# Two mixture-of-experts layers: token rows stored by chunk of channels, the second pair's token numbers by a product on chip, and another order of the last router logits

## The reference, cut to what matters

```python
group_idx = argmax(softmax(t @ w_router_group + b_group))         # one group for each token
in_group  = (t @ w_router_expert + b_expert)[group_idx]           # its 8 experts
top_p, top_i = top_k(softmax(in_group), 2)
gates = group_gate * top_p / sum(top_p)
# for each of the token's two experts e:
y[token] += gate * ((silu(x @ w_gate[e]) * (x @ w_up[e])) @ w_down[e])
```

## Time and profile before

| | |
|---|---|
| median of 3 runs | 2305.43 us (2302.77 to 2305.70) |
| profiled execution | 2309.89 us, its span 2307.7 us |
| PE busy | 2007.6 us, 87% of the span |
| mean granted TensorE clock | 0.938 of 2.4 GHz |
| chain that ended last | PE 38%, issue 32%, DMA 23%, DVE 4% |
| single largest DMA parts of it | in_w (layer 2's weights) 12%, y_rows stores 8% |

### The profile page before, as it was taken

The page is one execution under the profiler, slowest core; times in us unless marked ns, Lnnn a source line. Parts: engine busy times, 40 slices in busy tenths (PEclk is TensorE's granted clock), DMA queues, the critical chain, the costliest instruction groups (busy, mean ns, idle before and its releaser), DMA issues.

```text
span 2307.7 us, 22803 instructions
## 1 busy us (share of the span) xinstructions
PE 2007.6 (87%) x8418; PEld 1107.0 (48%) x8418; DVE 795.5 (34%) x1472; ACT 382.0 (17%) x663; POOL 80.6 (3%) x84
## 2 busy tenths in 40 slices
PE   6999998887863999999999999999988988778781
PEld 4543335554432666656557776666554322223220
DVE  3336524112114355555554554232251101111105
ACT  2335531000001122232211111111000000000000
POOL 0001010200001000000000000000001000000001
PEclk9999998899886999999999999999988998999996
DMA  7715104699986211111011214222349999999993
GB/s 223 217 38 158 55 1 146 229 419 420 419 361 197 75 55 55 45 55 51 1 62 64 80 44 155 73 73 73 128 174 332 379 427 427 427 427 426 426 411 121
DMA packets 185573, 458.47 MB, mean 199 GB/s; under 512 B 30575, under 2 KB 134767, under 8 KB 159404
## 3 DMA queue, kind: packets, MB, share of 16 engines
q1 hardware_dynamic: 171916, 441.64, 51.0%
q0 software_dynamic: 7424, 16.06, 1.9%
q10 hardware_dynamic: 6176, 0.02, 0.1%
HBM read 434.20 MB, written 32.60 MB: 202 GB/s over the span
## 4 chain that ended last, share of the span: by engine, by line
PE 38%; issue 32%; DMA 23%; DVE 4%; SPq 2%; POOL 1%; ACT 0%; DVEq 0%; POOLq 0%; ACTq 0%
DMA stream<-in_w 12%; PE bank L1522 8%; DMA y_rows<-work 8%; PE bank L1389 6%; PE bank L451 3%; PE bank L391 2%; PE bank L1527 2%; PE bank L1402 2%; PE bank L416 2%; PE bank L1564 2%; PE bank L1390 2%; PE bank L466 1%; PE bank L395 1%; SPq L1304 1%; PE bank L479 1%
## 5 line engine op out<-in xcount | busy, mean ns | idle before, releaser
L1389 PE MATMUL bank<-stream,work 128*64 128x256 f32 (+1 forms) x1072 | 379.6, 513 | 72.4 <-DMA stream<-in_w 56.5
L1390 PE MATMUL bank<-stream,work 128*64 128x256 f32 (+1 forms) x1072 | 380.1, 513 | 0.0
L1389 PEld LDWEIGHTS bank<-stream,work 128*64 128x64 f32 x1072 | 150.8, 143 | 248.1 <-issue 173.1
L1522 PE MATMUL bank<-hT,stream 128*128 128x512 f32 x512 | 230.4, 593 | 1.7 <-DVE hT L1019 1.7
L1402 PE MATMUL bank<-stream,work 128*64 128x512 f32 x736 | 192.2, 676 | 39.4 <-DVE work L1476 39.4
L1390 PEld LDWEIGHTS bank<-stream,work 128*64 128x64 f32 x1072 | 150.7, 143 | 41.3 <-issue 25.7
L1473 DVE TENSOR_TENSOR work<-bank,work 64x256 f32<-64x256 f32 (+1 forms) x68 | 37.6, 554 | 341.6 <-ACT work L1445 341.3
L1522 PEld LDWEIGHTS bank<-hT,stream 128*128 128x128 f32 x512 | 93.4, 190 | 99.9 <-issue 98.0
L1480 DVE COPY work<-bank 128x512 f32<-128x512 f32 x34 | 23.5, 692 | 325.8 <-DMA y_rows<-work 173.2
L1402 PEld LDWEIGHTS bank<-stream,work 128*64 128x64 f32 x736 | 60.6, 153 | 146.7 <-issue 121.1
L1841 PE MATMUL bank<-stream 128*128 128x256 f32 x480 | 113.1, 383 | 3.3 <-ACT work L1866 3.3
(11 more groups left out here) (358 smaller groups left out, 2550.4 us busy)
## 6 DMA issues: line engine op xcount, KB each, us to landing
stream<-in_w SPq DMA_DIRECT2D x99, 2048.0 KB, 20.2
stream<-in_w_in SPq DMA_DIRECT2D x68, 512.0 KB, 4.2
stream<-in_w_gate SPq DMA_DIRECT2D x34, 1024.0 KB, 13.3
stream<-in_w_up SPq DMA_DIRECT2D x34, 1024.0 KB, 17.7
stream<-in_w_down SPq DMA_DIRECT2D x26, 1024.0 KB, 22.5
y_rows<-work SPq DMA_DIRECT2D x136, 128.0 KB, 14.6
stream<-in_w_in SPq DMA_DIRECT2D x16, 1024.0 KB, 5.4
stream<-in_w_out SPq DMA_DIRECT2D x2, 4096.0 KB, 15.5
```

Source lines behind the costliest of these rows:

```text
L1389: pe.matmul(bank[2 + s][other:other + 64, 0:m.ff], tokens, m.wg[slot][:, k, :], start=k == 0, stop=k == KD - 1)
L1390: last = pe.matmul(bank[2 + s][mine:mine + 64, 0:m.ff], tokens, m.wu[slot][:, k, :], start=k == 0, stop=k == KD - 1)
L1522: last = pe.matmul(bank[4 + c % 2][:, :], w_hg[:, c, k, :], hT[:, k, :], start=k == 0, stop=k == KD - 1)
```

## The change

1. `x_rows` (and so `x_dram` and the gathered rows) holds the channels in the order (k, q) instead of (q, k), for channel q*8+k. All transposes and products that read it now read 128 floats side by side. DVE (layer 1) or ACT (layer 2, a new copy out of `xres`) writes it with a step of 128 floats.
2. `key` and `place` are also made for experts 2 and 3 (a second DVE operation of the same size). In the spread, after 8 products, 4 new products of one column each multiply the second half of `place` with the token numbers less 512. DVE adds 512 and casts at the end of its routing, and POOL issues the gather of pair 1 with these numbers after the fifth scatter (`FIRST_GATHER` is (1, 1)). The list then serves pairs 2 and on.
3. In layer 2, ACT copies `x_rows` and folds tiles 0 to 2; SP's store waits for ACT's copy. The logits are in the order 0, 1, 2, transposes of tile 3, logits 3. `x_rows` lies over `xg` and `xgT`, so the gather of pair 1 waits for the end of the spread there, and DVE's first copy into `xgT` for the landed stores.
4. `clear_dve` computes the token numbers, and no longer clears `xg` in layer 2.

```diff
@@ turn_rows_pe (the same slice in tokens_pe and, as stationary operand, in spread_pe)
-                    last = pe.transpose(bank[out_bank[i][h]][:, k * P:(k + 1) * P], moe1.x_rows[:, i, 4 * h + k:D:KD], ident[:, :])
+                    last = pe.transpose(bank[out_bank[i][h]][:, k * P:(k + 1) * P], moe1.x_rows[:, i, (4 * h + k) * P:(4 * h + k + 1) * P], ident[:, :])
@@ new
+        def fold_act(act, s, i):
+            for h in range(2):
+                act.wait_ge(tr_done, (s * NT + i) * 2 + h + 1)
+                act.activation(hT[:, 4 * h:4 * h + 4, i * P:(i + 1) * P],
+                               bank[4 + (i % 2) * 2 + h][:, :].rearrange("p (a b) -> p a b", a=NT), ACT.Copy).then_inc(hT_ready, 1)
@@ route_dve
-            step(dve.scalar_tensor_tensor(m.key, rank[:, :, 0:2], 1.0, m.aa[:, 0:NT, 0:2], ALU.add, ALU.mult))
-            dve.tensor_tensor(m.place, m.key.rearrange("p a b -> p (a b)").unsqueeze(2).to_broadcast([P, 2 * NT, SLOTS]),
-                              m.r_place.unsqueeze(1).to_broadcast([P, 2 * NT, SLOTS]), ALU.is_equal).then_inc(spread, 1)
+            step(dve.scalar_tensor_tensor(m.key, rank[:, :, 0:4], 1.0, m.aa[:, 0:NT, 0:4], ALU.add, ALU.mult))
+            for q in range(2):
+                dve.tensor_tensor(m.place[:, q], m.key[:, :, 2 * q:2 * q + 2].unsqueeze(3).to_broadcast([P, NT, 2, SLOTS]),
+                                  m.r_place.unsqueeze(1).unsqueeze(1).to_broadcast([P, NT, 2, SLOTS]),
+                                  ALU.is_equal).then_inc(spread, 1)
...
             dve.tensor_copy(m.blk_i[:, 0:SPARE + 1], m.blk[:, 0:SPARE + 1]).then_inc(routed, 1)
+            dve.wait_ge(*after(numbered, m.past + 1))
+            step(dve.tensor_scalar(m.first_f, bank[5][:, 0:1], float(SEQ), None, ALU.add))
+            dve.tensor_copy(m.first_i, m.first_f).then_inc(first_in[0], 1)
@@ route_pool
             for c in range(2):
                 for i in range(NT):
+                    if (c, i) == FIRST_GATHER:
+                        pool.wait_ge(*after(first_in, m.past + 1))
+                        pool.wait_ge(x_out, 16 * NT * (m.past + 1))
+                        pool.wait_ge(m.xt_done, m.past)
+                        gather_pool(pool, m, 1, m.first_i)
                     pool.indirect_dma_start(
                         out=m.list_dram, out_offset=bass.IndirectOffsetOnAxis(ap=m.dest_i[:, c * NT + i:c * NT + i + 1], axis=0),
                         in_=token[:, i:i + 1], in_offset=None).then_inc(listed, 16)
@@ clear_dve
             dve.memset(m.aa[:, NT, :], 0.0)
-            dve.memset(m.xg[:, :, :], 0.0)
+            dve.tensor_copy(m.number, token[:, :]).then_inc(*dve_own.up())
+            dve.wait_ge(*dve_own.now())
+            dve.tensor_scalar(m.number, m.number, float(SEQ), None, ALU.subtract).then_inc(*dve_own.up())
+            dve.wait_ge(*dve_own.now())
+            if m.layer == 1:
+                dve.memset(m.xg[:, :, :], 0.0)
@@ experts_pool
             pool.wait_ge(list_in, 16 * m.past + 16)
-            pool.wait_ge(x_out, 16 * NT * (m.past + 1))
-            for i in range(1, PAIRS_MAIN):
-                if i >= 2:
-                    pool.wait_ge(m.xt_done, i - 1)
+            for i in range(2, PAIRS_MAIN):
+                pool.wait_ge(m.xt_done, i - 1)
                 gather(i)
@@ spread_pe
             for k in range(KD):
+                if k == 2:
+                    pe.wait_ge(spread, m.past * 2 + 2)
+                    for i in range(NT):
+                        last = pe.matmul(bank[5][:, 0:1], m.place[:, 1, i].rearrange("p a s -> p (a s)"), m.number[:, i:i + 1],
+                                         start=i == 0, stop=i == NT - 1)
+                    last.then_inc(numbered[0], 1)
@@ out_pe
-            logits(0)
-            logits(1)
+            for i in range(NT - 1):
+                logits(i)
             transposes_pe(pe, s, NT - 1, norm_src, ready)
-            for i in range(2, NT):
-                logits(i)
+            logits(NT - 1)
@@ sync, layer 2
-                sp.wait_ge(ln_ready, i + 1)
-                sp.dma_start(moe2.x_dram[i * P:(i + 1) * P, :], xres[:, i, :]).then_inc(x_out, 16)
+                sp.wait_ge(x_laid, i + 1)
+                sp.dma_start(moe2.x_dram[i * P:(i + 1) * P, :], moe2.x_rows[:, i, :]).then_inc(x_out, 16)
@@ scalar, layer 2
                 root_tile_act(act, 5, i)
+                act.wait_ge(ln_ready, i + 1)
+                act.activation(moe2.x_wide[:, i], xres[:, i, :].rearrange("p (q k) -> p q k", k=KD), ACT.Copy).then_inc(x_laid, 1)
+                if i < NT - 1:
+                    fold_act(act, 3, i)
@@ vector, layer 1
-                dve.tensor_scalar(moe1.x_rows[:, i, :], xres[:, i, :], stat[:, i:i + 1], None, ALU.mult).then_inc(normed, 1)
+                dve.tensor_scalar(moe1.x_wide[:, i], xres[:, i, :].rearrange("p (q k) -> p q k", k=KD), stat[:, i:i + 1], None,
+                                  ALU.mult).then_inc(normed, 1)
```

More of the change, by code:

```diff
@@ L24 @@
 NO_TOKEN = 1 << 20
+FIRST_GATHER = (1, 1)
 A_HEADS, A_DIM = 8, 64
@@ L327, in build @@
         gains_in = sem("gains_in")
-        bias_in, spread, toep_in = sem("bias_in"), sem("spread"), sem("toep_in")
+        bias_in, spread, toep_in, x_laid = sem("bias_in"), sem("spread"), sem("toep_in"), sem("x_laid")
         w_pair_in = [sem("w_pair_in0"), sem("w_pair_in1")]
@@ L1063, in __init__ @@
                 m.y, at = cut(at, 2, D // 2)
-                m.place = m.y.rearrange("p a b -> p (a b)")[:, 0:2 * NT * SLOTS].rearrange("p (a s) -> p a s", s=SLOTS)
+                m.place = m.y.rearrange("p a b -> p (a b)").rearrange("p (q i a s) -> p q i a s", q=2, i=NT, a=2)
                 m.yg, at = cut(at, 2 * NT, D)
-                m.x_rows = m.yg[:, 0:NT, :] if layer == 1 else xres
-                m.key, at = cut(at, NT, 2)
+                m.x_rows = m.yg[:, 0:NT, :] if layer == 1 else work[:, pool_at:pool_at + NT * D].rearrange("p (a n) -> p a n", a=NT)
+                m.x_wide = m.x_rows.rearrange("p a (k q) -> p a q k", k=KD)
+                m.key, at = cut(at, NT, 4)
+                m.number, at = cut(at, NT)
+                m.first_f, at = cut(at, 1)
+                m.first_i, at = cut(at, 1)
                 m.lg, at = cut(at, NT, LOGITS)
@@ L1100, in __init__ @@
                 m.wd = [d.rearrange("p (c n) -> p c n", c=m.fc) for _, d in slots]
-                m.dest_i, m.blk_i, m.list_i = (x.bitcast(I32) for x in (m.dest_i, m.blk_i, m.list_i))
+                m.dest_i, m.blk_i, m.list_i, m.first_i = (x.bitcast(I32) for x in (m.dest_i, m.blk_i, m.list_i, m.first_i))
                 m.x_dram = nc.dram_tensor(f"x_rows{layer}", (SEQ, D), F32, kind="Internal").ap()
@@ L1220, in route_dve, with gather_pool @@
             dve.tensor_copy(m.blk_i[:, 0:SPARE + 1], m.blk[:, 0:SPARE + 1]).then_inc(routed, 1)
+            dve.wait_ge(*after(numbered, m.past + 1))
+            step(dve.tensor_scalar(m.first_f, bank[5][:, 0:1], float(SEQ), None, ALU.add))
+            dve.tensor_copy(m.first_i, m.first_f).then_inc(first_in[0], 1)
+        def gather_pool(pool, m, i, numbers):
+            pool.indirect_dma_start(
+                out=m.xg[:, i % 2, :], out_offset=None, in_=m.x_dram,
+                in_offset=bass.IndirectOffsetOnAxis(ap=numbers, axis=0),
+                bounds_check=SEQ - 1, oob_is_err=False).then_inc(m.xg_in[i % 2], 16)
         def route_pool(pool, m):
@@ L1337, in gather @@
             def gather(i):
[L1338 to L1341, removed]
+                gather_pool(pool, m, i, m.list_i[:, i:i + 1])
             pool.wait_ge(list_in, 16 * m.past + 16)
-            pool.wait_ge(x_out, 16 * NT * (m.past + 1))
-            for i in range(1, PAIRS_MAIN):
-                if i >= 2:
-                    pool.wait_ge(m.xt_done, i - 1)
+            for i in range(2, PAIRS_MAIN):
+                pool.wait_ge(m.xt_done, i - 1)
                 gather(i)
@@ L1371, in tokens_pe @@
             for k in range(KD):
-                last = pe.transpose(bank[k // 4][:, k % 4 * P:(k % 4 + 1) * P], m.xg[:, b, k:D:KD], ident[:, :])
+                last = pe.transpose(bank[k // 4][:, k % 4 * P:(k % 4 + 1) * P], m.xg[:, b, k * P:(k + 1) * P], ident[:, :])
             last.then_inc(m.xt_done, 1)
         def spread_pe(pe, m):
-            pe.wait_ge(spread, m.past + 1)
+            pe.wait_ge(spread, m.past * 2 + 1)
+            if m.layer == 2:
+                pe.wait_ge(x_laid, NT)
             for k in range(KD):
+                if k == 2:
[4 more added lines that the diff above has]
+                    last.then_inc(numbered[0], 1)
                 for i in range(NT):
-                    last = pe.matmul(bank[6 + k // 4][:, k % 4 * P:(k % 4 + 1) * P], m.x_rows[:, i, k:D:KD],
-                                     m.place[:, 2 * i:2 * i + 2, :].rearrange("p a s -> p (a s)"), start=i == 0, stop=i == NT - 1)
```

(5 more changed lines are left out.)

5 lines of the change are left out of this document (2 added, 3 removed).

## The result

The changed kernel takes **2313.16 us** (median of 20 runs, 2305.62 to 2328.03); the kernel before, on the same chip, takes 2303.39 (20 runs, 2298.16 to 2309.68). The ratio is 1.0048, 95% interval 1.0036 to 1.0061: slower by 0.5%. The forecast was 2287 in a range of 2278 to 2305, and faster by 0.8%. What came is rival B, the starved list, for which the prediction worked out 10.6 us of loss; 9.8 were measured.

What follows compares the result with a forecast made beforehand. The prediction took expert stages to be bound by moving weight bytes, with 10 and 18 us lost at the streams' starts. Gains of 6.1 and 12.5 us, total 18.6, against 2305.4 gave 2287, range 2278 to 2305.

Steps and rivals of the forecast that it cites:

- rival B: Experts of both layers: list waits until weights of pairs 0 and 1 drain; 2.5 and 8.1 us lost, 2316; chance 0.11.
- The step that failed: List's load beside the weights, both layers: scaled from the last scatter's 2.5 times, 12 us in layer 1, 9 in layer 2.
- The upper bound of the same paragraph: List's load: 193 packets for an engine; if each 8 pay 4.8 us, it lands only when the stream has run dry.
- The rule that spoke for it: DMA queues: engines switch after packets of some 9 to 17 descriptors, so 11 to 21 turns for the list.
- Pair 0 in layer 1: Start of layer 1's experts: first weights request at 417, down products done at 426.7, some 14 us earlier than before.
- the spread's pitch: Spread, both layers: stationary read's step sets 0.243 us a record; side by side 0.114 at 2.4 GHz, about 5 us gained each.
- The transposes: Transposes of rows, now read side by side: the sum takes no gain for them.
- DVE's write at a step of 128 floats: Layer 1's row write: between 0.75 and 1.6 us; +0.5 taken.
- The logits of layer 2: Routing of layer 2: 3.5 us after the last fold instead of 7.0; routing 0.9 to 3.7 earlier, 0.9 taken.
- POOL waited for the numbers: Early gather of pair 1: numbers don't delay POOL, its turn comes after five scatters at 413.9 and 1738.4.
- layer 2's sum: Layer 2's experts: bytes moved by 1796.4 instead of 1810, gain 13.6, less 1 for gaps: 12.5 us.
- the sum, had the list been short: Both layers' expert stages: gains of 6.1 us in layer 1 and 12.5 in layer 2, total 18.6.

Runs made afterwards that it cites:

- e2: The changed kernel with SP's first weights request in the experts' loop held until the list has been read; 2296.6 us, ratio 0.9968.
- e1: The changed kernel with the list laid out slot by pair, loaded as 128 runs of 96 bytes instead of 3072 of 4; 2287.8 us, ratio 0.9931.
- e8: The changed kernel with its old list loaded in two parts, 512 elements for pairs 0 to 3, then the other 2560; 2297.1 us, ratio 0.9964.
- e5: The kernel before with only the slot-by-pair list layout of e1; 2293.6 us, ratio 0.9947.
- e6: The list layout of e1 put into e4, without the new channel order and logits order; 2290.7 us, ratio 0.9937.
- e9: e1 with the list's load issued by POOL instead of ACT, in both layers; 2283.4 us, ratio 0.9908.
- e4: The kernel before with only the second place, the number product and the early gather of pair 1; 2294.7 us, ratio 0.996.
- e3: The changed kernel with pair 1 gathered by the list again, the number product kept but unused for the gather; 2325.6 us, ratio 1.0093.
- e7: e1 with SP requesting expert 1's weights before the last store of x_rows in layer 2; 2287.7 us, ratio 0.9923.

## Why the prediction was wrong

**The step that failed** is one term: "The nearest row for a small transfer beside the stream is the last scatter, 8.03 us against 3.24: 2.5 times. So I take 12 us in layer 1 and 9 in layer 2." It measured 30.6 and 31.4. A scatter is 8 packets for an engine, the list 193, and what the stream costs is a turn for each packet. So the list landed when the stream was over, at 449.6 and 1788.2, and pair 2 came 6.7 and 7.0 us later than before; with the weights held back instead (e2), the same 3088 packets landed in 4 us and the loss was gone. Scaling the list's own time by a scatter's factor compares two quantities of which only one counts packets. The upper bound of the same paragraph was the right form ("it lands only when the stream has run dry"), and I gave it 0.11 because "eight scatters in a row beside the stream landed at most 8 us after issue". Those eight count for little: by the turns of e1 and e8, 8 packets for an engine are 2 to 4 us of waiting, so they bound nothing for 193.

**The rule that spoke for it.** By the packets of the DMA view above, an engine changes queues after each packet. The Trainium skill, "DMA: Bandwidth & Descriptors", section "Queues, rings and completion order", has turns of typically 9 to 17 descriptors, and the prediction made 11 to 21 turns of it for this list. It pointed to the right rival, but the length of a turn differs from the measured one, and the measurement decides: one packet, so 193 turns.

**Rival B, by its own steps.** Layer 1: list at 449.3 (449.6 measured), transposes of pair 2 at 453.5 (454.77), next weights at 460 (462.17). Layer 2: transposes at 1798 (1799.2), weights again at 1809.6 (1812.26). Its losses were 2.5 and 8.1; by the table they are 5.2 up to the end of layer 1 and 4.7 behind the first scatter of layer 2. So layer 1 lost twice what was worked out, and layer 2 little more than half. The shares come from one execution of each kernel, both some 6.5 us above the medians, and are known to a few microseconds only. But that the sum came within a microsecond (10.6 against 9.8) is luck as much as working: the two errors cancel.

**What held of the other terms.**
- Pair 0 in layer 1: first request of weights at 416.91 (417 forecast), its down products done at 426.39 (426.7). In layer 2 1750.46 and 1767.89 (1747.3 and 1764.5), both late by less than the 5.4 us that the layer starts late.
- The stride of the stationary read sets the spread's pitch. The view of L1416 shows the loads' duration in ns (min/median/max), for L1380 before it was 336:

```profile
L1416 PEld LDWEIGHTS bank<-work x128: 192/192/338, 399.6 to 1741.5; 128*128 128x128 f32 x128
```

  But only at 2.4 GHz: at 1.2 the first 16 records of layer 1 keep a pitch of 0.224 us ((403.19 - 399.61)/16), hardly less than the 0.243 of before. And the granted clock rose 2 us later than before (after 407, not at 405.3), so 8 of 12 us ran at 1.2 GHz. The spread began 1.8 us earlier than I had it and ended at 411.75, where 411.7 was forecast: two errors that cancel, so the match is luck. In its own length it gains 3.4 us in layer 1 and 5.4 in layer 2; I took about 5.
- The transposes, whose moving operand was read at a step of 8 floats before and side by side now, gain nothing, as the sum had it: 8 of layer 1's logits take 1.05 us before and 1.04 after, both at 2.4 GHz.
- DVE's write at a step of 128 floats takes 1.35 us for 0.75: +0.6, where I took +0.5. ACT's copy takes 1.97 us for the 1.2 that I took:

```profile
L2543 DVE TENSOR_SCALAR work<-xres,stat x4: 1326/1348/1366, 355.1 to 377.4; 128x1024 f32<-128x1024 f32 x4
```

- The logits of layer 2: 48 records took 7.10 us, not 5.5. The clock fell within them (granted 0.90 of full speed over 1710 to 1712 and 0.50, that is 1.2 GHz, from 1712 on), so part of the upper bound came true. The first scatter of layer 2 comes 5.4 us later than before, of which 5.2 are layer 1's end: 0.2 later by itself, where I had 0.2 earlier (0.9 less 0.7). The table tells more. From the end of layer 1 to that scatter it is 1056.4 to 1058.7 us in the four kernels with the old order and 1055.3 to 1059.0 in the eight with the new one, so these traces show no gain of the new order at all.
- POOL waited for the numbers in neither layer (its gap ahead of the gather is the 0.30 us of every scatter). The gathers went out at 412.0 and 1744.25.
- A slip in layer 2's sum: 34.5 MB less 13.6 are 20.9, not 20.4, which makes the gain 12.4 and not 13.6. It changes nothing of the above.

**And the sum, had the list been short?** e1 is the kernel that I had in mind: 17.1 us less than before, where I forecast 18.6. By the table it ends layer 1 5.3 us earlier (6.1 forecast). Its rest is 14.7 shorter (12.5). As far as one execution of each kernel shows, the bookkeeping of the stream held, though by another list (6.1 us in layer 1 for the 12 assumed) and with pair 0 held up by ACT. But e5 shows that a part of this isn't the change's: e5 has the old spread, the old gather and only a short list with its scatters' new targets, and takes 11 of the 17 us. Numbers and the early gather add 3 to it (e6; the runs of e5 and e6 overlap), channels by chunk and the logits' order another 3 (e1), all of it in layer 2, and POOL's load of the list 4 (e9). These shares hold in this order only: without the short list, numbers and early gather are worth 10 (e4). The prediction never asked what a shorter list would be worth in the kernel before.

Open is why a load's first packet moves 2.5 to 3.3 us later beside the stream. No run takes the reordering of layer 2's logits apart from the channels' layout.

## What to carry to other kernels

Price a small transfer beside a stream by its packets: packets for an engine times the time of one packet of the stream, plus its quiet time and, here, 2.5 to 3.3 us more until its first packet moves. If that is longer than the stream lasts, the stream's end is the price. A change that makes work faster ahead of a bulk request also moves that request, so list every small transfer that it now overtakes, and cut its packets first (here 3072 runs of 4 bytes to 128 of 96). And look at what stands behind the wait for such a transfer on the issuing engine: moving the wait to an engine with nothing to do gained 4 us more.

## What the runs showed of the hardware

- Two queues that both have work share an engine packet by packet, whatever the size: 118 to 118 with mostly 16 KB against 4 bytes, 225 to 225 with mostly 8 KB, 173 to 173 in e8, and 15 to 15 within 0.55 us. On a quiet queue 2644 of the list's packets passed in 2 us (kernel before, 420 to 422), in the stream 118 in 4 us.
- The list's first packet moved 1.0 us after the issue on a quiet queue (kernel before, e2, e4, e5, e6), and 3.5 to 4.3 us after it beside the stream (changed kernel, e1, e3, e7, e8).
- Scatters of 4 bytes whose targets lie 96 bytes apart landed in 2.1 us (median, e5, layer 1), those to neighbouring places in 3.2 (median, kernel before, layer 1). I had not expected it, and no run takes it apart.
